# Expert loop of a mixture-of-experts stage: two lanes without the skew between pairs

## What is computed

```python
grp = argmax(xt @ rg_w + rg_b)                       # one of 4 groups
expert_logits = (xt @ re_w + re_b).reshape(T, 4, 8)  # 8 experts a group
top_val, top_idx = lax.top_k(expert_logits[arange(T), grp], 2)
gate = p_grp * softmax(top_val)
...
def expert_block(args):                  # for each block of rows of one expert
    xb, e = args
    a = xb @ w_gate[e]                   # 1024 x 512
    u = xb @ w_up[e]                     # 1024 x 512
    return (jax.nn.silu(a) * u) @ w_down[e]   # 512 x 1024
...
out = zeros((T, D)).at[slot_tok].add(ys * slot_gate)
```

## Time and profile before

| | |
|---|---|
| median of three runs | 2211.17 us |
| the profiled execution | 2204.74 us |
| its span | 2203.0 us |
| TensorE busy in the span | 2014.4 us (91%) |
| VectorE, ScalarE, GpSimd busy | 1014.5, 709.8, 86.7 us |
| mean granted TensorE clock | 0.967 of full speed |

### The profile page before, as it was taken

How to read it: one execution, slowest core, us unless ns; L and a number is a source line. 1 busy time by engine, 2 the same in 40 slices (tenths; PEclk the granted TensorE clock), 3 DMA queues, 4 the chain that set the end, 5 groups by cost and what they waited for, 6 DMA issues and landing times. The chain is left out here.

```text
span 2203.0 us, 27100 instructions
## 1 busy us (share of the span) xinstructions
PE 2014.4 (91%) x9747; PEld 1421.3 (65%) x9747; DVE 1014.5 (46%) x1706; ACT 709.8 (32%) x963; POOL 86.7 (4%) x181
## 2 busy tenths in 40 slices
PE   7989899999999999789999998999788989989885
PEld 5778678888888877578888887778443333333331
DVE  3553456555536555646555437888433111111114
ACT  3334414343322455514343323455311111111112
POOL 2001100000000000000000000000001000000001
PEclk9999999999999999899999999999998999999998
DMA  8232028542322422205332322411244999899996
GB/s 227 64 87 96 19 77 298 146 118 80 115 77 63 126 68 71 79 20 144 96 96 78 133 77 55 128 58 39 84 151 183 379 374 376 356 381 381 381 393 255
DMA packets 218108, 353.83 MB, mean 161 GB/s; under 512 B 12117, under 2 KB 174237, under 8 KB 196378
## 3 DMA queue, kind: packets, MB, share of 16 engines
q1 hardware_dynamic: 205418, 308.92, 40.3%
q0 software_dynamic: 10144, 34.67, 4.4%
q10 hardware_dynamic: 2448, 8.91, 1.0%
HBM read 326.21 MB, written 28.88 MB: 161 GB/s over the span
## 5 line engine op out<-in xcount | busy, mean ns | idle before, releaser
L1037 PE MATMUL PS<-XS,split 128*128 128x512 f32 (+1 forms) x2304 | 482.3, 372 | 3.6 <-DVE XS L154 3.1
L1037 PEld LDWEIGHTS PS<-XS,split 128*128 128x128 f32 x2304 | 406.5, 188 | 79.1 <-DVE XS L154 3.6
L154 DVE TENSOR_TENSOR split<-ring,split 128x2048 fp32r<-128x2048 f32 x110 | 251.7, 2290 | 274.7 <-ACT split L149 274.5
L2747 PE MATMUL PS<-moe_raw,moe_x 128*64 128x512 f32 x1152 | 278.2, 628 | 51.9 <-ACTq L2848 51.2
L149 ACT CAST split<-ring 128x2048 fp32r<-128x2048 f32 x110 | 209.5, 1905 | 197.0 <-PE PS L1073 110.8
L2747 PEld LDWEIGHTS PS<-moe_raw,moe_x 128*64 128x64 f32 x1152 | 82.1, 143 | 216.0 <-issue 169.4
L1073 PE MATMUL PS<-split,XS 128*128 128x512 f32 x672 | 152.6, 389 | 0.0
L1073 PEld LDWEIGHTS PS<-split,XS 128*128 128x128 f32 x672 | 126.2, 188 | 26.1
L2926 DVE COPY moe_h<-PS 128x256 f32<-128x256 f32 x36 | 15.3, 425 | 273.8 <-PE PS L2756 273.8
L2772 PE MATMUL PS<-moe_raw,moe_h 128*64 128x512 f32 x576 | 130.7, 596 | 0.6 <-issue 0.6
L1118 ACT ACTIVATE W<-PS,taps 128x512 f32<-128x512 f32 x88 | 67.2, 775 | 143.6 <-PE PS L1037 143.5
(11 more groups left out here) (441 smaller groups left out, 2417.6 us busy)
## 6 DMA issues: line engine op xcount, KB each, us to landing
moe_raw<-in_expert_w_gate SPq DMA_DIRECT2D x56, 1024.0 KB, 11.0
moe_raw<-in_expert_w_up SPq DMA_DIRECT2D x56, 1024.0 KB, 12.9
moe_raw<-in_expert_w_down SPq DMA_DIRECT2D x56, 1024.0 KB, 10.9
ring<-in_w_up SPq DMA_DIRECT2D x88, 512.0 KB, 5.2
ring<-in_w_down SPq DMA_DIRECT2D x44, 512.0 KB, 4.1
expert_rows<-rows POOLq DMA_DIRECT2D x3, 4096.0 KB, 26.2
ring<-in_w_in SPq DMA_DIRECT2D x24, 512.0 KB, 5.3
expert_rows<-W ACTq DMA_DIRECT2D x17, 512.0 KB, 8.5
```

The costliest lines, as they stand in the source:

```text
L154: return dve.tensor_tensor(lo, raw, hi.bitcast(F32), ALU.subtract)
L1037: mm = pe.matmul(PS[:, b + q, rows], w[:, c, q, :], x_half(k, high)[:, c, rows], start=(c == 0 and m == 0), stop=(c == KC - 1 and m == 2))
L2747: mm = pe.matmul(PS[64 * side:64 * side + 64, t, :], xT[:, at, 64 * t:64 * t + 64], raw[:, BUFFER[t], 2 * phase + side, 512 * c:512 * c + ...
```

## The change

It takes the skew away and moves three other things:

- TensorE: `pair` does lane 0 and lane 1 of a pair whole. Gate/up of lane 0, gate/up of lane 1 with lane 0's turn between, lane 0's down, lane 1's turn, the turning of the next pair's rows, lane 1's down.
- VectorE: copies in the same new order; the next pair's rows are copied after lane 1's middle.
- ScalarE: lane 1's result of the pair before is kept and saved first, then arrivals of B (lane 0) and A (lane 1) are waited for before lane 0's silu. In the first pair, both rows of pair 1 (`keep_rows(1, ...)`) stand behind the arrivals of lane 1's weights.
- The five transposes of the table's columns come right after the first gate/up product.

```diff
+        def pair(i, first=False, last=False):
+            if not first:
+                gate_up(i, 0, PHASE_A, 6 * i + 1)
+                gate_up(i, 0, PHASE_B, 6 * i + 2)
+            gate_up(i, 1, PHASE_A, 6 * i + 3)
+            turn_mid(i, 0)
+            gate_up(i, 1, PHASE_B, 6 * i + 4)
+            if last:
+                turn_gates()
+            if first:
+                pe.wait_ge(s.tabled, 1)
+            down(i, 0, 6 * i + 5)
+            turn_mid(i, 1)
+            if first:
+                pe.wait_ge(s.x_kept, 4)
+                turn_x(1)
+            elif not last:
+                turn_x(i + 1, 16 * i)
+            down(i, 1, 6 * i + 6)
+
...
         gate_up(0, 0, PHASE_A, 1)
-        rows_x(0, 1)
-        gate_up(0, 0, PHASE_B, 2)
-        turn_first(1)
         pe.wait_ge(s.summed, 1)
         for j in range(5):
             mm = pe.transpose(PS[0:32, 3, 192 + 64 * j:256 + 64 * j], spread[0:64, j, :], k.ident[0:64, 0:64])
         mm.then_inc(s.sums_turned, 1)
+        rows_x(0, 1)
+        gate_up(0, 0, PHASE_B, 2)
+        turn_first(1)
...
-        def body(i, last=False):
-            gate_up(i, 0, PHASE_A, 6 * i)
-            turn_mid(i - 1, 1)
-            gate_up(i, 0, PHASE_B, 6 * i + 1)
-            down(i - 1, 1, 6 * i + 2)
-            gate_up(i, 1, PHASE_A, 6 * i + 3)
-            turn_mid(i, 0)
-            gate_up(i, 1, PHASE_B, 6 * i + 4)
-            if last:
-                turn_gates()
-            else:
-                turn_x(i + 1, 16 * i)
-            down(i, 0, 6 * i + 5)
...
+        pair(0, first=True)
         with pe.Fori(1, end) as i:
-            body(i)
-        body(end, last=True)
-        turn_mid(end, 1)
-        down(end, 1, 6 * end + 6)
+            pair(i)
+        pair(end, last=True)
...
             a = (32,) if first else needs(2 * i)
+            b = (32, 32) if first else needs(2 * i + 1)
             if first:
+                weights_in(PHASE_A, b)
                 leave_first(1)
+            else:
+                keep(i - 1, 1)
+                save(i - 1)
+                weights_in(PHASE_B, a)
+                weights_in(PHASE_A, b)
             gate(i, 0)
+            weights_in(PHASE_B, b)
+            weights_in(PHASE_D, a)
             if first:
                 keep_rows(1, 0)
                 keep_rows(1, 1)
-            b = (32, 32) if first else needs(2 * i + 1)
-            weights_in(PHASE_A, b)
-            if not first:
-                keep(i - 1, 1)
-                save(i - 1)
-            weights_in(PHASE_B, b)
-            weights_in(PHASE_D, a)
             gate(i, 1)
+            weights_in(PHASE_D, b)
+            keep(i, 0)
             if first:
                 act.wait_ge(s.tabled, 1)
             if not last:
-                ahead = needs(2 * i + 2)
-                weights_in(PHASE_A, ahead)
-            keep(i, 0)
-            if not last:
-                weights_in(PHASE_B, ahead)
-            weights_in(PHASE_D, b)
+                weights_in(PHASE_A, needs(2 * i + 2))
...
             multiply(i, 0)
             if last:
                 late_tokens(dve)
             leave_mid(i, 0)
-            if not last:
-                leave_x(i + 1)
             multiply(i, 1)
             if last:
                 late_slots(dve)
...
+            leave_mid(i, 1)
+            if not last:
+                leave_x(i + 1)
```

More of the change, by code:

```diff
@@ L2933, in leave_x, with body @@
                    .then_inc(out, 1)
-        def body(i, first=False, last=False):
-            if not first:
-                leave_mid(i - 1, 1)
+        def body(i, last=False):
             multiply(i, 0)
@@ L2946, in body @@
                 late_slots(dve)
-        body(0, first=True)
+            leave_mid(i, 1)
+            if not last:
+                leave_x(i + 1)
+        body(0)
         with dve.Fori(1, end) as i:
@@ L2951, in experts_vector @@
         body(end, last=True)
-        leave_mid(end, 1)
     pairs = [W[:, 4096:6144], W[:, 6144:8192], raw[:, 0, 0, :], raw[:, 0, 1, :]]
```

## The result

| | before | changed |
|---|---|---|
| median, 14 runs each on one chip | 2210.60 us | 2199.19 us |
| lowest to highest | 2203.86 to 2213.78 | 2187.36 to 2205.89 |
| profiled execution | 2204.7 | 2197.57 (span 2195.8) |

The ratio is 0.9948, 95% interval [0.9937, 0.9960]: 11.4 us faster, where 31 were forecast, and 3 us outside the range of 2163 to 2196. The direction and the place were right, the size was not.

What follows compares the result with a forecast made beforehand. In the expert loop DMA and TensorE take turns being late, down weights waiting for down products. Loop -33.4, pair 16 to 17 +3.2, head 0, tail -1 sum to -31 us: 2178 us forecast, range 2163 to 2196.

Steps and rivals of the forecast that it cites:

- The hole at lane 1's D: DMA queue empty before lane 1's down weights; issued 12.4 us after lane 1's last gate/up product starts, closing it.
- D0 is what is late next: Lane 0's down weights for the next both-new pair, issued 30.5 us after lane 1's last gate/up product starts.
- The same chain of three pieces: From issue of lane 0's down weights to start of lane 1's last gate/up product: 20.55 us, giving period 51.05.
- rival 1: TensorE's clock falls at lane 1's first gate/up product in both-new pairs: 18 us back, 2192 up to 2198; 12%.
- Rivals 2 and 3: Transfers reach the byte floor, 11 us more, 2163, 8%; or the hole only moves, 2205 to 2211, 4%.
- floor of 49.5: A two-pair loop period's 21.0 MB at 424 GB/s needs 49.5 us; no new order can win more.
- rival 3: The hole only moves, opening 5.8 us wide at lane 0's down weights; period near 55.5, 2205 to 2211; 4%.
- Pair 16 to 17: Two both-new pairs ending the loop: 28.9 us before, 32.1 after, as their bytes need; loss 3.2 us.
- Tail: End of the kernel: pair 16's save no longer shares engines with the last down weights; -1 us, bounds -2 and 0.
- Head: Start of the expert loop: earlier table and first weight transfer buy nothing; 0 us, bounds -1.1 and +1.2.
- VectorE's copy as cover for d1: Turning x (1.1 us) covers VectorE's 0.42 us copy before lane 1's down product; 0.55 us of cover left.

Runs made afterwards that it cites:

- without the gathers: Changed kernel with the gathers of rows left out, so pairs from 2 on work on old rows and the result is wrong: 2163.95 us, single run.
- the other order of the pieces: Changed kernel with written-out constant loads, and in both-new pairs lane 1's gate/up weights ahead of lane 0's down weights: 0.979 of the kernel before, median 2163.58 us.
- x turned last: Changed kernel with the turning of the next rows moved behind lane 1's down product: ratio 0.9895 to the kernel before.
- half the down product: Changed kernel with two of four row blocks of each down product left out, so the result is wrong: 2164.14 us, single run.
- the early table alone: Kernel before, skew kept, with only the transposes of the table's columns moved up: ratio 1.0005 to the kernel before.
- the late table and the new loop: Changed kernel with the transposes of the table's columns back at their old place: ratio 0.9932 to the kernel before.
- the constants: SyncE's 26 loads written out with constant expert numbers and waits; in the changed kernel, same order of pieces, ratio 0.9932 to the kernel before.

## Why the prediction was right in kind and wrong in size

- *The hole at lane 1's D, and that the new order closes it*: right. It was issued 12.56 after S (12.4 forecast), and the slices of zeros are gone.
- *D0 is what is late next, at S+30.5*: right to the tenth, 236.8 us in seven periods.
- *"The same chain of three pieces ... 20.55 us. So the new period is 30.5+20.55 = 51.05 us"*: this is the step that failed, by 20.5 us over the loop. It is two terms. The chain from D0's issue to B's landing took 21.9, which is 9.2 in all, and S then came 1.6 after the landing, which is 11.3 in all.
- *The transfers' part of it.* The 20.55 were read at a D issued into a queue that had long been empty (the zeros of the strip before). In the new order both D's are issued about when the last transfers run out. What goes with that was seen above: dips at 250 to 380 GB/s that the busy share hides, so that 0.5 MB of earlier weights is still ahead of D0, and engines out of step, so that part of a later piece is paid for in the chain. In step and with the gather clear of the restart it is 20.2, in step with the gather on it 20.8, as it came 21.9. The term was that of a state of the queue which the change itself took away. The dips alone are not the cause: without the gathers D0 is issued at the same 30.5, dips of 184 to 393 GB/s are there too, and no chain was over 19.2. Why the engines leave step, and why it needs the gathers, no run shows; it stays open.
- *The clock's part of it* was rival 1, given 12%: 2.3 us at each both-new pair. g1A did slow down at all of them, behind waits of 4.0 to 6.0 us, and it cost 1.6 rather than 2.3, as B landed later too. The argument against it, short waits of 1.91 and 0.71 without a fall, said nothing of a wait of 5; and the trace of the kernel before had more to say: of its six waits of 2.85 to 2.91 us in front of g1A, four were followed by 5.06 to 6.67 us and two by 3.65. The wait itself was under-estimated (3 us) because of the short chain. Rival 1's time, 2192 to 2198, is what was measured (2199); half of that is its mechanism and half the chain.
The Trainium skill (TensorE: Matmul & The Clock Gate, section "HAM oscillation — how this bites in real kernels") says that matmuls waiting on DMA for too long at a stretch lose half the clock every time round the loop. The trace agrees here: seven waits of 4.0 to 6.0 us, seven products of 5.0 to 6.6 us.
- *Rivals 2 and 3*: the floor of 49.5 was not reached by this change, but by the other order of the pieces. The hole did move in part to lane 0's D, rival 3's place, as a dip of two slices.
- *Pair 16 to 17*: +2.0 for +3.2, right. *Tail*: -3.2 for -1. The last down product ends 12.7 after S(17) in both, so it lies behind it: the save of pair 16 has landed 9.5 us before S(17) where it landed 5.0 after, and GpSimd's first read of the saved rows goes out 4.6 after S(17) instead of 8.2. The kernels with the old order of products and pieces have tails of 40.8 to 41.7, those with the new order of products and the old of pieces (but for x turned last, 40.1, and half the down product, 37.9) 38.4 to 39.7.
- *Head*: 0 was taken, bounds -1.1 and +1.2; it is +2.9. The first D came 1.1 us earlier as forecast (30.4 after the first gate/up product, before 31.5), and by the order of the products: with the early table alone it was 32.1, with the late table and the new loop 29.8. But B landed 21.9 after it instead of 17.9. Without the gather the head is 49.7, so the gather in front of the weights, priced at 1.2, is 2.6 of it.
- *VectorE's copy as cover for d1*: right, there is no pause in front of d1. With x behind d1 there is one of 0.56, since the cover is gone, and it cost less than it gave.

## What to carry to other kernels

Split a chain's time into "issued to landed" and "landed to used" before reusing it: here one number, 20.55, hid both an empty queue and a full clock, and they were off by 1.3 and 1.6 us, seven times. When a period is set by a queue that is about to run dry, first look at the order of the requests: asking last for what frees last gave 31 us to the new loop, and 26 to the old one with the constants in it, more than any move of instructions. And read GB/s beside the DMA share; 0.98 busy was 9% short of full.

## What the hardware showed that was not expected

- A queue that just runs dry can cost more than one that stands clearly empty: chain 21.9 and three broad dips, against 20.2 and one deep dip with x turned last. Without the gathers it cost nothing (19.1, and 1.2 of bytes less).
- The 16 engines can leave step by a third of a 2 MB piece, and a transfer lands with the slowest: up to 2 us a chain, with the 16 steps of one landing spread over 2.7 us instead of 0.5.
- A gather of 0.5 MB is not free in an idle stretch: put into the hole of the kernel before, it made the loop 17 us slower and the whole 22.6 (1.2 us of bytes each).
- Busy share is no throughput: in the period from 1778 us the gathers' 1.05 MB took 6.2% of the engines' time, before 4.6%, at the same number of packets (288).
